# Last attention over six PSUM banks with three units in flight, head norms issued ahead of the Fourier stage, turned rows placed 64 bytes off a multiple of 128 bytes

## What is computed

```
px, pz = split_in(hx), split_in(hz)
a_x = fourier_mix(px['fourier'])                       # real part of a 2-D FFT
b_x = neighborhood_attention(na_q(px), na_k(px), ...)  # 4 heads, own tokens + context, with a bias
c_x = gla_output(ox_gla, px['gla_r'], gla_norm)        # gated linear attention
d_x = block_attention(qx_gqa, [kx_gqa, kz_gqa], ...)   # 4 heads, 2 key heads, own tokens + context
out_x = jnp.concatenate([a_x, b_x, c_x, d_x], axis=-1)
```

## Time and profile before

| | |
|---|---|
| median of 3 runs | 3516.27 us (3513.65 to 3518.14) |
| profiled execution, its own time | 3517.91 us |
| its span, first to last instruction | 3515.8 us |
| mean granted TensorE clock | 0.945 of 2.4 GHz |
| PE busy | 3237.6 us (92%), 23014 products |
| DVE, ACT, POOL busy | 1922.0, 1641.8, 152.6 us |
| read from memory | 552 MB, 157 GB/s over the span |

### The profile page before, as it was taken

How to read it: one execution, slowest core, us unless ns; L and a number is a source line. 1 busy time by engine, 2 the same in 40 slices (tenths; PEclk the granted TensorE clock), 3 DMA queues, 4 the chain that set the end, 5 groups by cost and what they waited for, 6 DMA issues and landing times. The chain is left out here.

```text
span 3515.8 us, 54378 instructions
## 1 busy us (share of the span) xinstructions
PE 3237.6 (92%) x23014; PEld 2949.5 (84%) x23014; DVE 1922.0 (55%) x2904; ACT 1641.8 (47%) x2444; POOL 152.6 (4%) x143
## 2 busy tenths in 40 slices
PE   6999899998999999999898778999999999999898
PEld 4899788897779998899798557999989898989797
DVE  5455465555546655555545325445575656566655
ACT  5444455544445444444444314435654444665343
POOL 0000000001000000000100100000110101101100
PEclk8999999998999999999999758999999999999899
DMA  6665344553435555765355303546435554434464
GB/s 217 204 217 178 130 144 156 192 180 113 124 123 189 168 184 180 235 204 167 110 162 171 114 12 117 183 144 194 126 109 191 168 186 156 147 116 134 155 196 138
DMA packets 464997, 556.67 MB, mean 158 GB/s; under 512 B 25285, under 2 KB 431733, under 8 KB 464373
## 3 DMA queue, kind: packets, MB, share of 16 engines
q1 hardware_dynamic: 464756, 553.20, 48.6%
HBM read 552.12 MB, written 1.05 MB: 157 GB/s over the span
## 5 line engine op out<-in xcount | busy, mean ns | idle before, releaser
L259 DVE TENSOR_TENSOR wl<-wr,wh 128x1024 fp32r<-128x1024 f32 x702 | 826.7, 1213 | 238.2 <-ACT wh L251 236.6
L251 ACT ACTIVATE wh<-wr 128x1024 fp32r<-128x1024 f32 x702 | 700.5, 1039 | 154.4 <-DMA wr<-in_ffn_w_dram 105.7
L116 PE MATMUL psum<-xt_hi,wh 128*128 128x256 f32 (+1 forms) x2000 | 576.9, 288 | 9.8 <-DVE xt_lo L2539 5.0
L117 PE MATMUL psum<-xt_lo,wh 128*128 128x256 f32 (+1 forms) x2000 | 569.5, 285 | 0.0
L118 PE MATMUL psum<-xt_hi,wl 128*128 128x256 f32 (+1 forms) x2000 | 569.5, 285 | 0.0
L1833 DVE TENSOR_TENSOR wl<-wr,wh 128x1024 fp32r<-128x1024 f32 (+3 forms) x336 | 388.9, 1197 | 94.0 <-ACT wh L1825 92.6
L116 PEld LDWEIGHTS psum<-xt_hi,wh 128*128 128x128 f32 (+1 forms) x2000 | 386.0, 193 | 18.7 <-issue 6.3
L117 PEld LDWEIGHTS psum<-xt_lo,wh 128*128 128x128 f32 (+1 forms) x2000 | 386.3, 193 | 2.2
L118 PEld LDWEIGHTS psum<-xt_hi,wl 128*128 128x128 f32 (+1 forms) x2000 | 385.9, 193 | 0.1
L116 PE MATMUL psum<-wh,xt_hi 128*128 128x256 f32 (+1 forms) x1280 | 376.9, 294 | 3.0 <-ACT vv L2945 1.5
L1825 ACT ACTIVATE wh<-wr 128x1024 fp32r<-128x1024 f32 (+3 forms) x336 | 322.7, 997 | 108.8 <-DMA wr<-in_mlp_w_dram 74.5
(11 more groups left out here) (444 smaller groups left out, 5716.9 us busy)
## 6 DMA issues: line engine op xcount, KB each, us to landing
wr<-in_ffn_w_dram SPq DMA_DIRECT2D x231, 1024.0 KB, 5.1
wr<-in_w_in_dram SPq DMA_DIRECT2D x88, 1024.0 KB, 5.1
wr<-in_w_mod_dram SPq DMA_DIRECT2D x72, 1024.0 KB, 4.9
wr<-in_mlp_w_dram SPq DMA_DIRECT2D x64, 1024.0 KB, 5.1
wr<-in_w_out_dram SPq DMA_DIRECT2D x20, 1024.0 KB, 5.0
wr<-in_mem_w_kv_dram SPq DMA_DIRECT2D x8, 1024.0 KB, 4.8
wr<-in_w_branch_dram SPq DMA_DIRECT2D x16, 512.0 KB, 3.5
wr<-in_w_branch_dram SPq DMA_DIRECT2D x8, 1024.0 KB, 4.8
```

What stands on the lines that cost most here:

```text
L116: pe.matmul(out, a[0], b[0], start=first, stop=False)
L117: pe.matmul(out, a[0], b[1], start=False, stop=False)
L251: act.activation(self.high[s][:, r], self.raw[s][:, r], ACT.Copy).then_inc(self.highs.sem, 1)
L259: dve.tensor_tensor(self.low[s][:, r], self.raw[s][:, r], self.high[s][:, r].bitcast(F32), ALU.subtract).then_inc(self.lows.sem, 1)
```

## The change

**A class `WideAttention`** takes the place of `HeadAttention` where `self.wide` is set, which is in layer 2. It has n + 3 steps for n units, 11 instead of 27. In step u PE writes the scores of unit u (bank u % 2), turns the probabilities of unit u - 2 (bank 2 + u % 2) and multiplies those of unit u - 3 with the values (bank 4 + u % 2). DVE masks unit u, scales u - 3 and takes the reciprocal for u - 1; ACT copies the turned u - 2, then takes the exponential of u. `masked` and `probs_t` have two places each, `inv` four. Z's last turn is waited for ahead of it, since it uses the same banks.

**Norms first**: at three places `norms()` stands before `spectral()` in the background list.

**Offsets**: `xt`, `zt`, `ot_diff`, `mem_t`, `mem_t2`, `merged` and `latents_t` start 64 bytes lower, `ot_mem` 64 bytes higher; the ring's places start 128 bytes lower. What the mixers place relative to `xt` and `zt` (`own(...)`) moves along by 64 bytes. `ot_mla`, the feed-forward parts' `gated` and the second part's `square` stay.

```diff
+RING_SHIFT, ROW_SHIFT = 1 / 8, 1 / 16
...
-        self.raw = [self.at(f"wr{s}", [P, CHUNK], F32, 16 * s) for s in range(RING)]
+        self.raw = [self.at(f"wr{s}", [P, CHUNK], F32, 16 * s - RING_SHIFT) for s in range(RING)]
...
+class WideAttention(HeadAttention):
+    def __init__(self, w, units, buf, before, mask=None):
+        super().__init__(w, units, buf, before, mask)
+        self.n_steps = self.n + 3
+
+    def pe(self, pe):
+        w, n, buf = self.w, self.n, self.buf
+        self.before(pe)
+        for bank in (4, 5):
+            w.open(pe, bank)
+            w.hold(bank, self.wait_done)
+        for u in range(n + 3):
+            if u < n:
+                un = self.units[u]
+                if u >= 2:
+                    pe.wait_ge(self.probs.sem, self.probs.at(u - 1))
+                for i, k in enumerate(un["keys"]):
+                    biased = un.get("bias") is not None and i == 0
+                    o = w.ps[:, u % 2, i * 256:(i + 1) * 256]
+                    last = pe.matmul(o, un["q"], k, start=True, stop=not biased)
+                    if biased:
+                        last = pe.matmul(o, un["bias"][0], un["bias"][1], start=False, stop=True)
+                last.then_inc(self.scores.sem, 1)
+            a = u - 2
+            if 0 <= a < n:
+                pe.wait_ge(self.probs.sem, self.probs.at(a + 1))
+                if a >= 2:
+                    pe.wait_ge(self.moved.sem, self.moved.at(a - 1))
+                m = self.width(a)
+                for i in range(m // P):
+                    last = pe.transpose(w.ps[:, 2 + a % 2, i * P:(i + 1) * P], buf["p"][:, a % 2, i * P:(i + 1) * P], w.eye)
+                last.then_inc(self.turned.sem, 1)
+            a = u - 3
+            if 0 <= a < n:
+                m, un = self.width(a), self.units[a]
+                pe.wait_ge(self.moved.sem, self.moved.at(a + 1))
+                if a >= 2:
+                    pe.wait_ge(self.done.sem, self.done.at(a - 1))
+                for i in range(m // P):
+                    last = pe.matmul(w.ps[:, 4 + a % 2, 0:HD], buf["pt"][:, a % 2, i * P:(i + 1) * P], un["v"][i], start=(i == 0),
+                                     stop=(i == m // P - 1))
+                last.then_inc(self.sums.sem, 1)
+            yield
...
+    def act(self, act):
+        for u in range(n + 3):
+            a = u - 2
...
+                act.wait_ge(self.turned.sem, self.turned.at(a + 1))
...
+                act.wait_ge(self.peaks.sem, self.peaks.at(u + 1))
...
+    def dve(self, dve):
+        for u in range(n + 3):
...
+                dve.wait_ge(self.scores.sem, self.scores.at(u + 1))
...
+                dve.wait_ge(self.sums.sem, self.sums.at(a + 1))
+                dve.tensor_scalar(self.units[a]["out"], self.w.ps[:, 4 + a % 2, 0:HD], inv[:, a % 4, 0:1], None,
+                                  ALU.mult).then_inc(self.done.sem, 1)
...
-    xt = [pair("xt", 80), pair("zt", 64)]
+    xt = [pair("xt", 80 - ROW_SHIFT), pair("zt", 64 - ROW_SHIFT)]
...
-            self.na = HeadAttention(w, units, self.buf, first if z else waits(first, bias_in.wait), None if z else self.mask)
+            kind = WideAttention if self.wide else HeadAttention
+            self.na = kind(w, units, self.buf, first if z else waits(first, bias_in.wait), None if z else self.mask)
...
-    background += [After(w, z_in.last)] + zm.spectral() + zm.norms() + zm.decays(z_in.gt) + zm.gla_out()
+    background += [After(w, z_in.last)] + zm.norms() + zm.spectral() + zm.decays(z_in.gt) + zm.gla_out()
...
-    background += xm1.attention(bias1, zk.na_turn.wait_done, zk.g_turn.wait_done)
+    background += xm1.attention(bias1, zk.na_turn.wait_done, zk.g_turn.wait_done, z_t9.wait_done)
```

More of the change, by code:

```diff
@@ L209, in at @@
     def at(self, name, shape, dt, kb):
-        return self.nc.alloc_sbuf_tensor_at(name, shape, dt, offset=self.base + int(kb * 1024))
+        return self.nc.alloc_sbuf_tensor_at(name, shape, dt, offset=self.base + round(kb * 1024))
     def share(self, name, n, unit=1):
@@ L3258, in first_block @@
              for kind, n in (("na", 8), ("gqa", 6), ("gla", 4))}
-    att = {k: small(f"head_{k}", 4) for k in ("neg", "sums", "inv")}
+    att = {k: small(f"head_{k}", 8) for k in ("neg", "sums", "inv")}
     assert small_kb[0] <= 185
@@ L3282, in first_block @@
     rep = lambda g, l, n: g[l:l + 1].unsqueeze(1).to_broadcast([P, n, HD])
-    streams = [Stream(w, s, x[:, 2 * s:2 * s + 2, :], c["ss"][s], xt[s], (80, 64)[s], (112, 130.5)[s], h[s]) for s in range(2)]
+    streams = [Stream(w, s, x[:, 2 * s:2 * s + 2, :], c["ss"][s], xt[s], (80 - ROW_SHIFT, 64 - ROW_SHIFT)[s], (112, 130.5)[s], h[s]) for s in range(2)]
     X, Z = streams
@@ L3332, in __init__ @@
             self.na_t = own(s, l, "na_t", [P, 4, TOK], 8)
-            self.buf = dict(att, p=own(s, l, "probs", [P, 2, 512], 0), sm=own(s, l, "masked", [P, 512], 4), pt=own(s, l, "probs_t", [P, 512], 6))
+            self.wide = l == 1
+            self.buf = dict(att, p=own(s, l, "probs", [P, 2, 512], 0))
+            if self.wide:
+                self.buf.update(sm=own(s, l, "masked", [P, 2, 512], 4), pt=own(s, l, "probs_t", [P, 2, 512], 12))
+            else:
+                self.buf.update(sm=own(s, l, "masked", [P, 512], 4), pt=own(s, l, "probs_t", [P, 512], 6))
             for k in att:
@@ L3422, in attention @@
                     units.append(u)
-            self.gqa = HeadAttention(w, units, self.buf, waits(self.g_turn.wait_done, self.na.wait_done))
+            self.gqa = kind(w, units, self.buf, waits(self.g_turn.wait_done, self.na.wait_done))
             self.turn = MixTurn(w, mix, s.pair, waits(self.gqa.wait_done, self.gla_norm.wait_done, self.fourier.wait_done), lambda eng: None)
@@ L3498, in first_block @@
     body[0].fetch += [xm.dft_in.fetch, xm.gla_in.fetch]
-    background += [After(w, x_in.last)] + xm.spectral() + xm.norms() + xm.decays(x_in.gt)
+    background += [After(w, x_in.last)] + xm.norms() + xm.spectral() + xm.decays(x_in.gt)
     background += xm.gla_out(zm.st.wait_done, dqi=xm.dqi, state=state) + xm.head_turns()
@@ L3544, in first_block @@
     xf3.pieces[6].fetch.append(xm1.gla_in.fetch)
-    background += [After(w, x_in1.last)] + xm1.spectral() + xm1.norms() + xm1.decays(x_in1.gt) + xm1.head_turns()
+    background += [After(w, x_in1.last)] + xm1.norms() + xm1.spectral() + xm1.decays(x_in1.gt) + xm1.head_turns()
     z_r3 = Residual(w, zf3, rows1, zf3.down[4].rows_in, Z.x, Z.ss, rtmp)
@@ L3602, in first_block @@
     order += x_out1.pieces
-    sq_x3 = Squares(w, waits(x_out1.wait_added, z_t9.wait_done), X.x, X.ss)
+    sq_x3 = Squares(w, waits(x_out1.wait_added, xm1.turn.wait_done), X.x, X.ss)
     x_t9 = turn(X, 1, 6, sq_x3.wait_squares, 3)
```

64 lines of the change are left out of this document (50 added, 14 removed).

## The result

The changed kernel takes 3390.9 us (median of four runs, 3383.6 to 3406.5) against 3517.2 us: the ratio is 0.965, with a 95% interval from 0.961 to 0.968. Forecast were 3414 us and a gain of 102; measured are 126. Run again beside three experiments it gave 3390.5 us, ratio 0.966 (0.964 to 0.968). The profiled execution took 3383.6 us (span 3381.5), 134 less than that of before.

What follows compares the result with a forecast made beforehand. The prediction took TensorE (PE), busy 92% of 3515.8 us, as the bound. Attention -28, norms -28 and offset -46 sum to -102 from 3517.9 us, giving 3416, or 3414 as a median; range 3355 to 3485.

Steps and rivals of the forecast that it cites:

- the forecast's own case (3395 to 3440): Whole kernel: the offset worth about half, time between 3395 and 3440 us; chance 0.33.
- the attention of 99 us at a clock near 0.5: Last attention, sign of being right: about 99 us from first neighbourhood score to first turn of the mixed rows.
- Attention, -28: Last attention: reordered units hide PE's waits, idle falling from 29.5 us to 1.5, for -28 us.
- I take the clock as it is: Last attention: the clock stays nearly all at 1.2 GHz, since gapless stretches did not lift it.
- The rival of the clock that comes up: Last attention: denser work lifts the clock, up to 48 us more off the forecast, 3366 us; chance 0.08.
- Norms, -28: Three Fourier places: norms first cut waits for `dft_ch` (-16.6) and the memset (-17.2), less a +6 charge: -28 us.
- The charge of 6 us for late splits: Three Fourier places: DVE runs two norms ahead of the next chunks' splits, charged 2 us a place, +6.
- Offset, -46: 256-wide chunk products: turned rows 64 bytes off save 3.7 ns on each of 12,300 products, -46 us.
- the weights' ring moves by 128 bytes and keeps its phase: 512-wide products: the ring's move should leave their pace at 226 ns.
- the prediction's estimate of 135 us: 256-wide products: 13,056 brought to the skill page's 109 ns would be worth some 135 us, more than any row supports.
- The offset does nothing: 256-wide products, rival: the streams never met, the extra 13 ns belong to changing the stationary operand; 3460 us, chance 0.29.
- slower than before: Feed-forward 256-wide products, rival: turned rows now meet the weight stream, +79 us less 56, 3539 us; chance 0.10.

Runs made afterwards that it cites:

- e8: Changed kernel with the last attention in its old form and PE's waits filled with six unread products a unit: 3499.3 us, ratio 0.996.
- e2: Changed kernel with only its last attention back in the old form, one unit in flight: 3453.1 us, ratio 0.982.
- e6: Changed kernel with ring and turned rows both 64 bytes off a multiple of 128: 3436.3 us, ratio 0.979.
- e5: Changed kernel with the tiles behind the ring 128 bytes higher, so `gated` and `square` lie 256 bytes off the ring's phase: 3402.1 us, ratio 0.967.
- e1: Changed kernel with both shifts, of ring and turned rows, set to 0: 3421.4 us, ratio 0.973.
- e10: Changed kernel with two more modulation chunks brought into the last attention, one every 4 steps in place of 6: 3380.1 us, ratio 0.961.
- e9: Changed kernel with the last two modulation chunks between the attention's units moved behind the output projection; one still fell between units: 3413.8 us, ratio 0.971.

## Why the prediction was right

The sum was right within 24 us of 126, and the overlap, the norms and the 256-wide pace were right as mechanisms. But part of that is luck: two terms erred by much in opposite directions, the attention by 34 us too little, the offset by 15 too much. The time of 3391 us also lies just under the forecast's own case (3395 to 3440), in none of the cases named. Of the signs that it set for being right, the attention of 99 us at a clock near 0.5 (66.7 us at 0.80) and `gated` unchanged at 226 ns (233) failed.

**Attention, -28, measured 62.** The mechanism and the size of the overlap were right: 27.1 us of standing are gone, no value product waits, and 2.5 us stay (1.5 forecast). What failed is the sentence "I take the clock as it is". It rested on a stretch without gaps that stayed at 1.2 GHz. That observation was sound, as e8 confirms. But I read it as "no clock in this attention" and overlooked the chunks. The kernel before already showed a rise in one, at 2014 us, in the rows between those I had chosen. The prediction also speaks of four modulation chunks between the units. The trace has two there, 18 us apart; in the changed kernel it is two again, 15.5 us apart, and the clock is up for more than half of the attention (most of 1974 to 2011 us): 33.4 us. So it isn't more chunks or much closer ones that gave this. What e2 shows is that the new form gave it, with the same chunks. Why the clock stays up longer in it, its order of products or its missing waits, is open. The rival of the clock that comes up (3366, up to 48 us off) had the place right and 0.08 as its chance. It gave density as the reason. e8 refutes that density alone does it, and not that it helps.

**Norms, -28, measured 32.6.** Left of the waits: 5.6 us forecast as 4.5, and 6.3 as 6. The waits alone give 32.4 us. The charge of 6 us for late splits doesn't show (waits for `wl` 12.7 us against 14.1). Within the spread of the runs that charge is what lies between 28 and 33.

**Offset, -46, measured 30.5.** The 256-wide products gained 3.6 ns where 3.7 was taken from `silu`, on 14,893 products where I counted 12,300: 53 us. That the two paces agree is luck. `silu` doesn't move. In e6 the ring does, to a multiple of 128 bytes from the start that the prediction works out for `silu`. The products of `silu` come every 114.6 ns there, where the full operands at such a distance take 119.6. So its pace says little about theirs, as the prediction's doubt had it. The step that failed is "the weights' ring moves by 128 bytes and keeps its phase, so 512-wide products should stay at 226 ns". The phase is one of 256 bytes for them (228.1 ns at 0, 233.1 at 128, 227.4 at 256 in e5), they went to 233, and 12 us were given back. The paces account for 41 us, the profiled executions of e1 and of the changed kernel differ by 33.7 (spans 3415.2 and 3381.5), the medians by 30.5. Of the 7 us between the first two, some 3 lie in 512-wide products outside the 250 ns and some 3 in those of `silu`; I have not followed them further. In the prediction's estimate of 135 us the factor is 12,300 products and not the 13,056 that it names; nothing else uses it.

**The rivals.** "The offset does nothing" is refuted by e1. The Trainium skill's rule in "SBUF — State Buffer", section "Who interferes with whom", by which PE has two independent read ports and waits on nobody, would have left the paces alone. Here the same instructions take 119.7 or 116.1 ns by the distance of the two operands alone. Whether the two reads meet or something else makes the difference, no run shows. The "slower than before" case expected a loss on the 256-wide products. There was a loss, but on the 512-wide ones.

## What to carry to other kernels

Where a dense stretch runs some ns above the pace its clock gives, move one operand's tile by 64 bytes and measure every width of product: 256-wide and 512-wide ones want different distances, and a tile that makes room for another changes its own. Work that stays at the low clock can be helped by what is put between it: two more chunks of the products that lift the clock were worth 10 us inside the attention rather than behind it (e10). Other spacings weren't tried. And where a forecast says "the clock stays", look for the one place where it rose.

## What the runs showed of the hardware

- The pace of back-to-back products depends on the distance between the starts of the two operands in a partition. 256-wide with 128-column operands: 119.5 to 119.7 ns at 0 bytes modulo 256, 117.4 at 32, 116.1 to 117.0 at 64 and 192, 118.5 at 128 (`ot_mla` alone). 512-wide: 227.4 to 228.1 ns at 0 modulo 256, 233.1 to 233.4 at 32, 64 and 128. Why the two differ in sign is open.
- Within one distance two paces occur: at 64 bytes stretches of 113 and of 118 ns, each kept over whole chunks. What picks between them is open.
- PE busy 114.8 of 118.0 us stayed at a clock of 0.50 (e8). Of the rises in the attention all but one (e9, at 2032.5 us) lie in a modulation chunk or less than 1 us behind it. What in a chunk does it wasn't tried.
